# First gathers ahead of the decode root, tile 0 turned beside the decode output, and a new order of the last sums

## The chip, the cores and the metric

The kernel runs as one program on 1 core of a Trainium2 chip. The metric is the device time of an execution in microseconds. TensorE (PE) multiplies; PEld is its loading of stationary operands; VectorE (DVE), ScalarE (ACT) and GpSimd (POOL) work elementwise; SyncE (SP) issues DMAs. Each engine runs its own instructions in order, and the engines meet at semaphores.

## What is computed

One step of a hybrid decoder layer for a prompt of 1024 tokens and 8 decode rows with 8192 cached positions each. What matters here is its second half:

```python
x = x + jnp.concatenate([attn, s5_out], axis=-1) @ w_out
x = x + hier_moe(rmsnorm(x, ln2_g), w_router_group, b_router_group, ...)
y_prompt = rmsnorm(xp, ln_f_g)          # and y_sample for the decode rows

# hier_moe: softmax over 4 groups, the best group; in it the best 2 of 8 experts
for e in range(N_EXPERTS):              # 32 experts, each 1024 -> 256 -> 1024
    he = jax.nn.silu(t @ w_gate[e]) * (t @ w_up[e])
    out = out + comb[:, e:e + 1] * (he @ w_down[e])
```

The attention of a decode row is normalized per head (the "decode root" below is its inverse square root), and the normalized and scaled heads go through `w_out`.

## The kernel before

The first part is a plan: `streams` lists units of work (such as `("V", ...)`, a group of cache pages), each with a cost and with the units it waits for. `make_plan` puts them in one order, and `banks` gives each unit that writes PSUM one of 6 banks in turn. Every engine then runs its part of the units in the plan's order, with a few moved by hand: `DVE_PLAN` and `POOL_PLAN` are these orders for VectorE and GpSimd, `PE_PLAN` for TensorE.

The plan ends thus. The prompt tokens are routed (`pick1`, `pick2`, `rank`, `rt0`, `rt1`, `ids`, `lists`, `spread`, `route`) while the last cache pages of the decode rows are read. `route` on VectorE writes `idc`, the row numbers of the first tiles, and signals `s_route`. The decode rows come last: `ov` 7, `dout` (the heads' sums of squares; `root` on GpSimd, L576, raises them to -0.5), `dout2` (scaled heads into `xm`), `out` NT (product with `w_out` on TensorE, L1856, added on VectorE at L1491), `hn` (mean square on ScalarE and VectorE, root on GpSimd), `hs` (L1504: normalized rows into `h2`), `hT` (8 turns on TensorE at L2182, copied with the ln2 scale on VectorE at L1512 beside the 96 rows of expert tile 0 and of tile 1).

The experts run in steps of one tile each: 96 gathered token rows and the 8 decode rows, through one expert. GpSimd gathers rows from `h2_scratch` with three indirect DMAs (`gather`, L694) into `hg[v % 2]`; VectorE turns and scales them (`scale`, L1749 and L1752) into `hgT[v % 2]`; TensorE multiplies gate and up (16 matmul instructions of 512 columns); ScalarE takes the tanh (L974); VectorE finishes the gated product (L1774, L1776); TensorE turns it (L2249) and multiplies down (8 instructions). Weights of a tile are loaded by SyncE (L529, L530) into one of four buffers as soon as the down product of the tile four before has read it. Tile v of the first round is `gather(0, v)` and `scale(0, v)`.

Before the change the first list is `lists` in GpSimd's order, put right behind `dout`: it waits for pages, clears `hg[0]` (L707), drains, waits for `s_route` and gathers tile 0. Tile 1 is gathered after all units (L722 to L726): wait for all pages, clear `hg[1]` (L723), drain, gather. On VectorE `turn0` (= `scale(0, 0)`) stands behind `hs` of the decode rows, and so ahead of their `hT`. `scale(0, 1)` follows all units.

At the end the two expert outputs of each token lie in `y_scratch`. SyncE waits for `s_stored` (ScalarE's signal that all scatters have landed) and loads tile after tile (L548, two loads of 512 KB each, 8 tiles of 128 tokens). For each, `combine` adds the weighted outputs to the residual `x1`: VectorE with two instructions (L1825) in tiles 0, 1, 4, 7 and the decode rows; for tiles 2, 3, 5 and 6 (`on_pe`) TensorE sums them with diagonal weights (4 matmuls of 512 columns, which are 8 instructions) and VectorE adds the sum (L1820). ScalarE squares, VectorE takes the mean, GpSimd the root (L749), VectorE normalizes (`normed`, L1838), SyncE stores (L552, L554). All engines take the tiles in the order 0 to 8, where 8 is the decode rows.

Of the kernel before, what the change touches and what calls it, by code (L numbers as in the profile page):

```python
# [9 lines left out]
NT = SEQ // 128  # L10
# [49 lines left out]
def psum_keys(unit):  # L60
# [18 lines left out]
        "dout": [(("dss",), 1)], "dout2": [(("drep",), 1)], "rank": [(("rank",), 1)], "ids": [(("ids",), 1)], "spread": [(("sp",), 1)],  # L79
# [3 lines left out]
def streams():  # L83

    dec = [(("dprep",), 2.5, [(("dq",), 6.0)])]
    for x in range(NPASS):
# [6 lines left out]
        for y in range(SPP):  # L93
# [9 lines left out]
            (("out", NT), 4.0, [(("dout2",), 1.0), (("out", NT - 1, 1, 1), 0.0)]), (("hn", NT), 0.0, [(("out", NT), 2.0)]),  # L103
# [151 lines left out]
def hymba_step(nc, io):  # L255
# [29 lines left out]
    with ctx:  # L285
# [120 lines left out]
        on_pe = [2, 3, 5, 6]  # L406
# [87 lines left out]
        def _(sp):  # L494
# [50 lines left out]
            sp.wait_ge(s_stored, 1)  # L545
            for i in range(NT):
                for c in range(2):
                    sp.dma_start(yg[i][c], io["y_scratch"][SEQ * c + 128 * i:SEQ * c + 128 * i + 128, :]).then_inc(f_g[i], 16)  # L548
            for i in range(NT + 1):
                sp.wait_ge(f_out, i + 1)  # L550
# [8 lines left out]
        def _(gp):  # L559
# [145 lines left out]
            def lists():  # L705
# [8 lines left out]
            todo = {"stats": stats, "dprep": dprep, "dkv": dkv, "dk2": dk2, "u": u, "k": k, "v": v, "O": O, "dout": dout,  # L714
                    "bU": bU, "bK": bK, "bH": bH, "bS": bS, "ld1": ld1, "ld2": ld2, "ld3": ld3, "hn": hn, "hs": hs,
                    "route": lists}
# [29 lines left out]
            def inv_rms(i):  # L746
                gp.wait_ge(f_ms, i + 1)
# [3 lines left out]
            for i in range(NT + 1):  # L751
                inv_rms(i)
# [10 lines left out]
        def _(act):  # L763
# [250 lines left out]
            for i in range(NT + 1):  # L1014
                act.wait_ge(f_x, i + 1)
                r = 128 if i < NT else NB
                act.activation(yb[i % 2][0:r, :], x1[0:r, i, :], ACT.Square, accum_out=st[0:r, i:i + 1]).then_inc(f_sq, 1)
# [3 lines left out]
        def _(dve):  # L1021
# [808 lines left out]
            def mean(i):  # L1830
                dve.wait_ge(f_sq, i + 1)
# [3 lines left out]
            def normed(i):  # L1835
                r = 128 if i < NT else NB
                dve.wait_ge(f_rs, i + 1)
# [4 lines left out]
            for i in range(NT + 1):  # L1842
# [5 lines left out]
            mean(NT)  # L1848
            normed(NT - 1)
            normed(NT)  # L1850


        @block.tensor
        def _(pe):
# [339 lines left out]

            def rank_():
# [210 lines left out]
```

## Time and profile before

| | us |
|---|---|
| median of 3 runs (lowest to highest) | 1426.63 (1423.94 to 1430.79) |
| profiled execution | 1422.35 |
| its span | 1420.7 |
| TensorE busy | 1261.7 (89%) |
| VectorE busy | 566.6 (40%) |
| GpSimd busy | 284.9 (20%) |
| ScalarE busy | 247.1 (17%) |

The profile has one line for a group of instructions: start and length in us, engine, line of the kernel, operation, the tile written and the tiles read, their shapes and the count; in square brackets how long the engine sat idle before, and what ended that. "PEclk" is the clock that TensorE was granted, 1.00 being 2.4 GHz and 0.50 being 1.2 GHz. Lengths of matmuls are modelled at their ends. Its mean over the execution is 0.949.

### The profile page before, as it was taken

The numbers are of one execution on the slowest core, as the hardware profiler recorded it, in microseconds if no ns is written. First come the engines' busy times: TensorE is split into PE (matmuls) and PEld (weight loads), VectorE is DVE, ScalarE is ACT, GpSimd is POOL, SyncE is SP. The second block draws the span as 40 slices with busy tenths as digits, with TensorE's granted clock in tenths as the row PEclk, the third lists the DMA queues.
The fourth block names the chain that finished last, engine by engine and source line by source line (L and its number), as shares of the span: only waits on it lengthen the run. The fifth ranks groups of instructions, "written<-read, shape, count | busy, mean of one in ns | idle before, by whom it ended". The sixth has DMA issues, their size and how long they took to land.

```text
span 1420.7 us, 26426 instructions
## 1 busy us (share of the span) xinstructions
PE 1261.7 (89%) x8778; PEld 633.6 (45%) x8778; DVE 566.6 (40%) x1452; ACT 247.1 (17%) x476; POOL 284.9 (20%) x395
## 2 busy tenths in 40 slices
PE   7999898999869988998887999996699999999944
PEld 4545565654324435666663444433234443443411
DVE  2723535343374556454441111216253332333317
ACT  3101121131112323332320100000011111111112
POOL 2003231232200200000010000000334544444311
PEclk9999999999999999999899999996699999999987
DMA  9998989778977999999998899899959999999736
GB/s 372 324 336 270 338 263 308 259 219 308 330 249 243 316 372 336 384 326 331 314 356 331 294 307 318 306 343 326 370 202 344 355 362 350 355 363 345 286 123 256
DMA packets 184178, 443.66 MB, mean 312 GB/s; under 512 B 26453, under 2 KB 26897, under 8 KB 175506
## 3 DMA queue, kind: packets, MB, share of 16 engines
q1 hardware_dynamic: 163602, 390.21, 77.4%
q0 software_dynamic: 20480, 52.12, 10.3%
q8 instruction: 66, 1.08, 0.3%
q14 instruction: 30, 0.25, 0.1%
HBM read 418.77 MB, written 30.65 MB: 316 GB/s over the span
## 4 chain that ended last, share of the span: by engine, by line
PE 67%; DMA 12%; issue 8%; DVE 5%; SPq 4%; DVEq 1%; POOL 1%; ACT 1%; POOLq 0%; ACTq 0%
PE WA L1856 52%; PE SC L1856 7%; PE OD L1856 5%; DMA ring<-in_cacheK 5%; SPq L513 4%; DMA ring<-in_cacheV 3%; DMA ring<-h_scratch,idc 2%; DMA arena<-in_x_s 2%; PE WA L1975 1%; DVE st L1163 1%; DMA arena<-y_scratch 1%; DVE arena L1838 1%; PE WA L2182 0%; DMA rope<-in_rope 0%; DVE arena L1179 0%
## 5 line engine op out<-in xcount | busy, mean ns | idle before, releaser
L1856 PE MATMUL WA<-arena 128*104 128x512 f32 (+11 forms) x1440 | 350.2, 427 | 21.9 <-issue 7.2
L1856 PE MATMUL WA<-arena,xm 128*128 128x512 f32 (+3 forms) x828 | 320.4, 582 | 8.4 <-DMA arena<-in_w_out 6.6
L1856 PEld LDWEIGHTS WA<-arena 64*128 64x128 f32 (+4 forms) x1440 | 182.6, 187 | 173.2 <-issue 149.5
L1856 PEld LDWEIGHTS WA<-arena,xm 128*128 128x128 f32 (+1 forms) x828 | 127.1, 175 | 165.6 <-issue 157.3
L576 POOL TENSOR_TENSOR st<-st,consts 128x1 f32<-128x1 f32 (+2 forms) x18 | 13.7, 763 | 499.1 <-DVEq L1197 279.2
L1856 PE MATMUL WA<-xm,arena 128*128 128x512 f32 (+1 forms) x192 | 87.0, 601 | 1.7 <-ACT arena L979 1.3
L1856 PE MATMUL OD<-ring,sall 128*32 128x512 f32 x512 | 69.5, 653 | 17.4 <-DMA ring<-in_cacheV 17.4
L1856 PE MATMUL OD<-ring,qpad 128*32 128x128 f32 x2048 | 66.3, 280 | 11.5 <-DMA ring<-in_cacheK 11.4
L1856 PE MATMUL SC<-ring,qpad 128*32 128x128 f32 x2048 | 65.1, 279 | 8.9 <-DMA ring<-in_cacheK 8.8
L1856 PEld LDWEIGHTS OD<-ring,qpad 128*32 128x32 f32 x2048 | 55.1, 112 | 31.6 <-issue 16.5
L1856 PEld LDWEIGHTS SC<-ring,qpad 128*32 128x32 f32 x2048 | 55.1, 112 | 24.4 <-issue 12.0
L1856 PE MATMUL SC<-ring,sall 128*32 128x512 f32 x512 | 61.4, 598 | 1.5 <-DMA ring<-in_cacheV 1.5
L849 ACT ACTIVATE arena<-WA,st 128x128 f32<-128x128 f32 (+7 forms) x64 | 47.4, 740 | 80.0 <-DVEq L1167 78.0
L1856 PE MATMUL WA<-xm 128*104 128x512 f32 (+1 forms) x132 | 58.3, 593 | 0.0
L1749 DVE STREAM_TRANSPOSE xm<-ring 128x768 f32<-128x768 f32 x16 | 25.1, 1570 | 83.0 <-DMA ring<-h_scratch,idc 83.0
L1856 PE MATMUL WA<-ring,xm 128*104 128x512 f32 x128 | 57.7, 605 | 0.0
L694 POOL DMA_INDIRECT ring<-h_scratch,idc x48 | 52.0, 1082 | 22.3 <-issue 17.6
L1485 DVE TENSOR_TENSOR arena<-arena,WA 128x512 f32<-128x512 f32 x16 | 11.0, 688 | 111.7 <-PE WA L1856 86.3
L694 POOL DMA_INDIRECT qpad<-h_scratch,idc x48 | 51.1, 1065 | 21.6 <-issue 21.6
L1856 PEld LDWEIGHTS WA<-xm,arena 128*128 128x128 f32 (+1 forms) x192 | 34.7, 186 | 45.9 <-issue 44.4
L1749 DVE STREAM_TRANSPOSE arena<-qpad 128x768 f32<-128x768 f32 x16 | 25.1, 1567 | 68.9 <-DMA qpad<-h_scratch,idc 68.9
L1163 DVE TENSOR_REDUCE st<-WA 128x1 f32<-128x128 f32 (+7 forms) x64 | 48.5, 758 | 5.1 <-issue 0.4
(372 smaller groups left out, 1238.8 us busy)
## 6 DMA issues: line engine op xcount, KB each, us to landing
ring<-in_cacheK SPq DMA_DIRECT2D x512, 256.0 KB, 4.6
ring<-in_cacheV SPq DMA_DIRECT2D x512, 256.0 KB, 4.7
arena<-in_w_gu SPq DMA_DIRECT2D x16, 2048.0 KB, 8.8
arena<-in_w_dn SPq DMA_DIRECT2D x16, 1024.0 KB, 11.8
ring<-in_w_gu SPq DMA_DIRECT2D x8, 2048.0 KB
xm<-in_w_gu SPq DMA_DIRECT2D x8, 2048.0 KB, 9.5
ring<-in_w_dn SPq DMA_DIRECT2D x8, 1024.0 KB
xm<-in_w_dn SPq DMA_DIRECT2D x8, 1024.0 KB, 13.1
```

The source lines that it names most:

```text
L513: sp.dma_start(ring[:, GRP * half + j, :], cache[bass.ds(pages[j], 1), :, :] .rearrange("a p n -> p (a n)")).then_inc(s_pg[PARTS * half + ...
L576: gp.tensor_tensor(x, x, consts[0:x.shape[0], C_NH:C_NH + 1].to_broadcast(list(x.shape)), ALU.pow).then_inc(s_rs, 1)
L694: gp.indirect_dma_start(hg[v % 2][:, 256 * b:256 * b + 256], None, io["h2_scratch"], bass.IndirectOffsetOnAxis(ap=idc[:, 3 * v + b:3 * v + ...
L849: act.activation(P[:, n % 2, c, 0:w], slot("S", i, h, c)[:, 0:w], ACT.Exp, bias=st[:, 4 * (n % 2) + c:4 * (n % 2) + c + 1], scale=HD ** -0 ...
L1163: dve.reduce_max(st[:, 8 + c:9 + c], S[:, 0:w], AX)
L1485: dve.tensor_tensor(q, q, slot("o", i, a)[:, :], ADD)
L1749: dve.transpose(rows_.rearrange("p k (b j) -> p k b j", b=3), hg[v % 2].rearrange("p (b j k) -> p k b j", b=3, k=KD)).then_inc(m_T, 1)
L1838: dve.scalar_tensor_tensor(x1[0:r, i, :], x1[0:r, i, :], st[0:r, i:i + 1], lnf[0:r, :], MUL, MUL)\
L1856: return pe.matmul(out, lhsT, rhs, start=first, stop=last, **kw)
L1975: last = pe.transpose(slot("AT", i, h)[:, 128 * j:128 * j + 128], P[:, n % 2, 0, 128 * j:128 * j + 128], ident)
```

## The change

Four edits and what belongs to them. (1) GpSimd takes the first list where the plan has `route`, ahead of `dout`; the list for tile 1 becomes a unit `next` right behind `dout`, without the drain: a semaphore says when the clearing is done. (2) VectorE takes `turn0` right behind `dout2`, ahead of the decode output's add. (3) A new unit `warm` puts five matmuls of identity by constants behind the decode output's product on TensorE, into a bank of its own (it counts as 4.0 us in the plan), and five more stand before the last sums, after the load of tile 0. Their results are not used. (4) The last tiles run in the order `TAIL` on all engines, and SyncE waits for the scatters itself in place of `s_stored`. The banks of the units behind `warm` stay what they were, as a unit of two banks follows it and starts at an even bank either way.

```diff
-            (("out", NT), 4.0, [...]), (("hn", NT), 0.0, [(("out", NT), 2.0)]),
+            (("out", NT), 4.0, [...]), (("warm",), 4.0, [(("out", NT), 0.0)]), (("hn", NT), 0.0, [(("out", NT), 2.0)]),
...
-                {("lists",): [u, ("route",)], ("hs", NT): [u, ("turn0",)]}.get(u, [u])]
-
-    POOL_PLAN = [x for u in PLAN if u != ("route",) for x in ([u, ("route",)] if u == ("dout",) else [u])]
+                {("lists",): [u, ("route",)], ("dout2",): [u, ("turn0",)]}.get(u, [u])]
+
+    POOL_PLAN = [x for u in PLAN for x in ([u, ("next",)] if u == ("dout",) else [u])]
...
-        on_pe = [2, 3, 5, 6]
+        on_pe, TAIL = [2, 3, 5, 6], [0, 1, 4, 2, 3, 5, 6, 7, NT]
...
-            sp.wait_ge(s_stored, 1)
-            for i in range(NT):
+            for n in range(2):
+                sp.wait_ge(m_st[n], 32 * n4)
+            for i in TAIL[:NT]:
...
+            def second():
+                gp.wait_ge(s_pgfree, RING // QP + NB * 2 * NPAGE // QP)
+                gp.memset(hg[1], 0.0).then_inc(s_qbd, 1)
+                gp.wait_ge(s_qbd, 4)
+                gather(0, 1)
+
...
-            gp.wait_ge(s_pgfree, RING // QP + NB * 2 * NPAGE // QP)
-            gp.memset(hg[1], 0.0)
-            gp.drain()
-            gather(0, 1)
...
-            for i in range(NT + 1):
+            for n, i in enumerate(TAIL):
                 combine(i)
-                if i >= 1:
-                    mean(i - 1)
-                if i >= 2:
-                    normed(i - 2)
...
+                if n >= 1:
+                    mean(TAIL[n - 1])
+                if n >= 2:
+                    normed(TAIL[n - 2])
...
+            def warm():
+
+                vacant(pe, "warm")
+                for n in range(5):
+                    last = mm(slot("warm")[:, :], ident, consts[:, 0:512])
+                    if n == 0:
+                        last.then_inc(full_sem("warm"), 1)
+                last.then_inc(free_sem("warm"), 1)
+
...
+
+            pe.wait_ge(f_g[0], 48)
+            for n in range(5):
+                mm(W[2][:, 0:512], ident, consts[:, 0:512])
             for n, i in enumerate(on_pe):
```

The waits and counts of ScalarE, VectorE, GpSimd and TensorE in the tail go by a tile's place in `TAIL` accordingly.

## Rows read from the trace of the kernel before

**Rows 1.** Chain of waits, steady expert steps: start us, us, what
```profile
1046.48 10.30 PE WA L1856 x24
...
1056.97 10.30 PE WA L1856 x24
```

**Rows 2.** Timeline by start: end of prompt rows, decode root, first expert
```profile
948.94 0.75 DVE L1504 TENSOR_SCALAR arena<-arena,st 128x1024 f32<-128x1024 f32 x1 [0.71 <-POOL st L576]
...
1002.21 0.56 POOL L576 TENSOR_TENSOR st<-st,consts 32x1 f32<-32x1 f32 x1 [51.61 <-DVEq L1259]
...
1011.29 1.70 DVE L1491 TENSOR_TENSOR arena<-arena,WA 8x256 f32<-8x256 f32 x4 [6.43 <-PE WA L1856]
...
1015.19 1.20 DVE L1504 TENSOR_SCALAR arena<-arena,st 8x1024 f32<-8x1024 f32 x1 [0.72 <-POOL st L576]
...
1016.48 1.04 PE L2182 MATMUL WA<-consts,arena 8*128 8x8 f32 x8 [5.33 <-DVEq L1505]
...
1021.14 0.22 DVE L1512 TENSOR_TENSOR arena<-WA,colw 128x64 f32<-128x64 f32 x1
...
1021.54 9.84 PE L1856 MATMUL WA<-arena 128*104 128x512 f32 x16 [4.02 <-DVEq L1515]
```

**Rows 3.** Timeline: route, first gathers, turn of tile 0
```profile
996.73 0.17 DVE L1740 CAST idc<-qpad 128x12 uint32<-128x12 f32 x1
...
1008.59 1.13 POOL L694 DMA_INDIRECT qpad<-h_scratch,idc  x1 [5.13 <-issue]
...
1011.35 1.01 POOL L694 DMA_INDIRECT qpad<-h_scratch,idc  x1 [0.30 <-issue]
...
1018.50 1.55 DVE L1749 STREAM_TRANSPOSE arena<-qpad 128x768 f32<-128x768 f32 x1 [2.11 <-DMA qpad<-h_scratch,idc]
...
1020.77 1.22 POOL L694 DMA_INDIRECT ring<-h_scratch,idc  x1 [0.31 <-issue]
```

**Rows 4.** Timeline of the tail: sums of the last tiles
```profile
1379.05 2.65 DVE L1825 SCALAR_TENSOR_TENSOR arena<-arena,wts 128x1024 f32<-128x1024 f32 x2 [18.31 <-DMA arena<-y_scratch]
...
1385.57 2.05 PE L1856 MATMUL WA<-arena,ring 128*128 128x512 f32 x2 [17.76 <-DMA arena<-y_scratch]
...
1390.91 1.22 DVE L1820 TENSOR_TENSOR arena<-arena,WA 128x1024 f32<-128x1024 f32 x1 [4.69 <-PE WA L1856]
...
1404.27 1.22 DVE L1820 TENSOR_TENSOR arena<-arena,WA 128x1024 f32<-128x1024 f32 x1
...
1415.91 2.47 DVE L1838 SCALAR_TENSOR_TENSOR arena<-arena,st 128x1024 f32<-128x1024 f32 x2
```

**Rows 5.** Windows of 1 us: window, length, busy per engine, granted clock, DMA, GB/s
```profile
1010.00:1011.00 1.00, 1.00 (x23) 0.32 (x12) 0.00 (x0) 0.00 (x0) 0.97 (x1) 1.00 0.90 385
...
1014.00:1015.00 1.00, 0.00 (x0) 0.00 (x0) 0.15 (x1) 0.29 (x2) 0.41 (x1) 0.50 1.06 402
...
1034.00:1035.00 1.00, 0.98 (x3) 0.69 (x4) 0.77 (x1) 0.34 (x1) 0.90 (x1) 0.50 0.43 123
```

**Rows 6.** Timeline: first gated product and second gate and up product
```profile
1031.41 0.38 ACT L974 ACTIVATE arena<-WA 104x256 f32<-104x256 f32 x1 [17.12 <-PE WA L1856]
...
1032.96 0.41 DVE L1774 SCALAR_TENSOR_TENSOR arena<-arena,WA 104x256 f32<-104x256 f32 x1
...
1034.39 8.48 PE L1856 MATMUL WA<-ring,xm 128*104 128x512 f32 x16
```

**Rows 7.** Load at 1377.4 of source line L548: its instruction and landing time
```profile
L548 SPq DMA_DIRECT2D arena<-y_scratch x1: 458/458/458, 1377.4 to 1377.4; - x1
...
DMA to landing us min/median/max: 10.5/10.5/10.5
```

**Rows 8.** All gathers, source line L694: time to landing
```profile
DMA to landing us min/median/max: 2.1/6.8/11.8
```

**Rows 9.** Timeline of SyncE: weight issues of two steps in the loop
```profile
1203.72 0.33 SPq L529 DMA_DIRECT2D xm<-in_w_gu  x1
...
1215.49 0.34 SPq L529 DMA_DIRECT2D arena<-in_w_gu  x1
```

More of the change, by code:

```diff
@@ L78, in psum_keys @@
         "hT": [(("hT",) + a, 2)], "r": [(("r",) + a, 1)],
-        "dout": [(("dss",), 1)], "dout2": [(("drep",), 1)], "rank": [(("rank",), 1)], "ids": [(("ids",), 1)], "spread": [(("sp",), 1)],
+        "dout": [(("dss",), 1)], "dout2": [(("drep",), 1)], "rank": [(("rank",), 1)], "ids": [(("ids",), 1)], "spread": [(("sp",), 1)], "warm": [(("warm",), 1)],
     }.get(k, [])
@@ L102, in streams @@
     dec += [(("dout",), 0.1, [(("ov", NB - 1), 1.0)]), (("dout2",), 0.2, [(("dout",), 2.0)]),
-            (("out", NT), 4.0, [(("dout2",), 1.0), (("out", NT - 1, 1, 1), 0.0)]), (("hn", NT), 0.0, [(("out", NT), 2.0)]),
+            (("out", NT), 4.0, [(("dout2",), 1.0), (("out", NT - 1, 1, 1), 0.0)]), (("warm",), 4.0, [(("out", NT), 0.0)]), (("hn", NT), 0.0, [(("out", NT), 2.0)]),
             (("hs", NT), 0.0, [(("hn", NT), 2.5)]), (("hT", NT), 1.0, [(("hs", NT), 0.8)]),
@@ L712, in lists @@
                 gather(0, 0)
+            def second():
[3 more added lines that the diff above has]
+                gather(0, 1)
             todo = {"stats": stats, "dprep": dprep, "dkv": dkv, "dk2": dk2, "u": u, "k": k, "v": v, "O": O, "dout": dout,
                     "bU": bU, "bK": bK, "bH": bH, "bS": bS, "ld1": ld1, "ld2": ld2, "ld3": ld3, "hn": hn, "hs": hs,
-                    "route": lists}
+                    "route": lists, "next": second}
             for unit in POOL_PLAN:
@@ L746, in inv_rms @@
             def inv_rms(i):
-                gp.wait_ge(f_ms, i + 1)
+                gp.wait_ge(f_ms, TAIL.index(i) + 1)
                 x = st[:, i:i + 1]
                 gp.tensor_tensor(x, x, consts[:, C_NH:C_NH + 1], ALU.pow).then_inc(f_rs, 1)
-            for i in range(NT + 1):
+            for i in TAIL:
                 inv_rms(i)
@@ L1011, in _ @@
             act.nop().then_inc(s_stored, 1)
-            for i in range(NT + 1):
-                act.wait_ge(f_x, i + 1)
+            for n, i in enumerate(TAIL):
+                act.wait_ge(f_x, n + 1)
                 r = 128 if i < NT else NB
-                act.activation(yb[i % 2][0:r, :], x1[0:r, i, :], ACT.Square, accum_out=st[0:r, i:i + 1]).then_inc(f_sq, 1)
+                act.activation(yb[n % 2][0:r, :], x1[0:r, i, :], ACT.Square, accum_out=st[0:r, i:i + 1]).then_inc(f_sq, 1)
         @block.vector
@@ L1841, in _ @@
             dve.wait_ge(f_gf, 16)
-            for i in range(NT + 1):
+            for n, i in enumerate(TAIL):
                 combine(i)
-                if i >= 1:
-                    mean(i - 1)
-                if i >= 2:
-                    normed(i - 2)
-            mean(NT)
-            normed(NT - 1)
-            normed(NT)
+                if n >= 1:
+                    mean(TAIL[n - 1])
+                if n >= 2:
+                    normed(TAIL[n - 2])
+            mean(TAIL[NT])
+            normed(TAIL[NT - 1])
+            normed(TAIL[NT])
         @block.tensor
@@ L2231, in _ @@
                     "dout": dout, "dout2": dout2, "bP": bP, "bK": bK, "bX": bX, "bY": bY, "glu": glu, "out": out_, "hT": hT,
-                    "r": r_, "rank": rank_, "ids": ids_, "spread": spread}
+                    "r": r_, "rank": rank_, "ids": ids_, "spread": spread, "warm": warm}
             for unit in PE_PLAN:
```

8 lines of the change are left out of this document (4 added, 4 removed).

## The prediction

> **What bounds the kernel now.** I read the 40 slices of the page first: TensorE is busy nearly throughout, and the change works where it is not: in the stretch from about 990 to 1046 us between the last pages of the cache and the steady run of experts, and in the last 50 us. The chain of waits then shows what stands between: from 1046 us on it is TensorE alone, 24 matmuls of 512 columns in 10.30 us each step, 0.43 us apiece [rows 1], so every microsecond by which the first step starts sooner should reach the end. Ahead of it I followed the timeline by engine. The decode root's chain is a row of short steps over all engines: GpSimd's power at 1002.21, the output product of the 8 decode rows, whose result VectorE adds from 1011.29, GpSimd's power again, the normalized rows (L1504, 1015.19, 1.20 us), eight turns on TensorE from 1016.48 for 1.04 us, then VectorE's copy at 1021.14 and the first expert's gate and up product at 1021.54 [rows 2]. Between 1017.52 and 1021.14 that chain stands still. Its engine, VectorE, is turning expert tile 0 from 1018.50 (`turn0`), and that waited for gathers of which the first went out at 1008.59 only [rows 3]. So the late gather sets the start of the experts. The tail is a chain on VectorE: it sits idle 4.69 us before 1390.91 for TensorE's sum of tile 2, and from there to the end it hardly rests [rows 4].
>
> **Gathers ahead of the decode root, and the turn beside the output product.** The route is ready at 996.90 (end of the cast into `idc`), yet GpSimd takes the first list after the root at 1002.21, then clears the target, and the gather starts 5.13 us after the clearing [rows 3]. After the change the clearing is done long before the route is there (GpSimd idles 51.61 us before 1002.21 [rows 2]), and GpSimd waits at the route. I take its start at 997.5. The last of three gathers began 1011.35 - 1008.59 = 2.76 us after the first and took 1.01 [rows 3], so they end near 1001.3, and the root at 1002.21 isn't held. The turn began 9.9 us after the first gather's start (1008.59 to 1018.50) [rows 3], and weights filled the queues then as they will now; so it can begin at 1007.4. It lasts with its scaling 2.64 us (1018.50 to 1021.14) [rows 2, 3], to 1010.1, before the product's result at 1011.29. Its cover is VectorE's idle time of 6.43 us before that row [rows 2]. VectorE's copy then follows the turns on TensorE directly: 1017.52 + 0.10 = 1017.62 in place of 1021.14, **3.52 us** sooner. The second list's clearing and gathers stand where the first ones stood; its stall of 5.13 us goes too if it belongs to the drain, which this list no longer has. Nobody needs it before the first gate and up product ends.
>
> **A clearing that leaves the chain.** L1504 took 0.75 us for 128 rows of 1024 at 948.94, but 1.20 for 8 rows at 1015.19 [rows 2], while GpSimd cleared the second target (it starts right after the power that released L1504). That clearing now runs right behind the first power. I count **0.45 us**. The Trainium skill, SBUF — State Buffer, section Who interferes with whom, says that VectorE in its two-port modes and GpSimd hold one port pair exclusively, and the trace agrees with these 0.45 us. By the same page the change has a debit: the second gathers, from about 1004, run beside the root's last small VectorE steps, and if a gather held the pair, one of 1.01 us could be added and the sum would be 9.4. The row at hand shows the gather and not VectorE lengthened (1.22 for 1.01) [rows 3], so I add nothing.
>
> **Five matmuls behind the output product (`warm`).** The granted clock is 1.00 (2.4 GHz) when that product ends and 0.50 (1.2 GHz) at 1014 after idling; the first gate and up product then takes 9.84 us for 16 matmuls, where 16 x 0.43 = 6.88 [rows 2, 5]. The clock is at 0.50 again at 1034, and the second product takes 8.48 [rows 5, 6]. `warm` is 10 matmul instructions, 4.3 us at the high clock, from 1011.2 to 1015.5, inside the wait for L1504, and delays nothing; at the low clock it would be 8.6 us to 1019.8, and the eight turns would be 3.3 us late. I take the first since the clock was high there. Most is saved if the clock then stays: 9.84 - 6.88 = **2.96**, and 8.48 - 6.88 = **1.60** for the second product. Between `warm` and the first product about 2 us remain with little in them, and 2 us between the two products; one fall costs what the second product shows, 1.60. I count one: **-1.60**.
>
> **The second tile is no longer waited for.** VectorE turned tile 1 when its gather landed, and only after it took the gated product: ScalarE's tanh began at 1031.41 and lasted 0.38, but L1774 ran at 1032.96 [rows 6]. With tile 1 turned before 1021, L1774 can follow 0.47 us after the tanh's start, at 1031.88: **1.08 us**.
>
> Head: 3.52 + 0.45 + 2.96 + 1.60 - 1.60 + 1.08 = 8.0 us. Bounds: no fall 9.6; two falls 6.4. The steps after it are TensorE's at 10.48 each and pass it on. The weights are asked for by the step itself, and tiles 2 and 3 are asked for at the same event as before.
>
> **The tail.** TensorE's sum of tile 2 began at 1385.57 at the low clock (the first two matmuls 2.05 us), and VectorE had it at 1390.91: 5.34 us, where 8 x 0.43 + 0.2 = 3.64 [rows 4]. In the new order tile 2 is loaded fourth. The load in that place (its second half issued 1377.4, landed after 10.5) is there at 1387.9 [rows 7], so TensorE starts 2.3 us later than now. Tile 0 is there at 1379.0, and the new five matmuls run from then, 4.3 us at the high and 8.6 at the low clock, so they end by 1387.6, before the load. If the clock is high then, VectorE has tile 2 at 1391.5, tiles 3, 5 and 6 each 3.44 later, tile 6 at 1401.85 instead of 1404.27 [rows 4]: **2.4 us**. VectorE fills the wait with tile 4 (two steps, 2.65 us), which it no longer does between tiles 3 and 5; what is left behind tile 6 is the same work as before (14.1 us, to 1418.38). With the low clock at the start 1.7 us of it go back: 0.7. Letting SyncE wait for the scatters itself saves one hop, under 0.1, taken as nothing.
>
> Sum: 8.0 + 2.4 = 10.4 us. The profiled execution, 1422.35 (span 1420.7), would come to 1411.9. It lies 4.3 us under the median of the runs, 1426.63; taken from that, 10.4 gives **1416.2**.
>
> **Rivals.** *The clock isn't kept* at either place: `warm` ends 2 us too soon and the tail's matmuls stop before tile 2 is there. Head 3.52 + 0.45 + 1.08, tail 0.7: 5.8 us, 1420.9. For it: the clock fell within 3 us of the output product's end [rows 5]. Against it: the gap left is shorter. *The root queues behind the gathers*: the stall of 5.13 us comes with the first gather and not with the drain, so the gathers end at 1006.3 and the power is 4.1 us late: 6.3 us gained, 1420.3. Against it: later gathers follow at once. *The turn blocks the output*: VectorE waits in `turn0` with the decode output behind it. A gather landed after 11.8 us at most [rows 8]; from 1000.2 that is 1012.0, the add starts at 1014.65, 3.4 late: 7.0 gained, 1419.6. It is also the case in which the change doesn't do what it says. *Slower*: steady steps miss their gathers. The step that asked for weights at 1203.72 was followed by the next at 1215.49, 11.77 us and not 10.48, as its tile had landed late [rows 9]. If the new start moved gathers against weight bursts, each missed step costs 1.29; from 8 missed steps of some 28 the gain is gone, and 20 give 25.8 - 10.4 = 15.4 us more, 1442.0. Against it: gathers and weights are both issued by the step, so their distance in time doesn't move.
>
> **How the numbers follow.** Forecast 0.60 (1414 to 1419), clock not kept 0.20, root queued 0.06, turn blocked 0.08, missed steps 0.06. A change under about 0.5% (7.1 us) can't be told from none here; the limit is 1419.5. The forecast's case lies mostly below it, the middle three mostly above: faster 0.64, same 0.30, slower 0.06. Range: no fall and a little luck of the runs, 12.0 + 2.7, gives 1411.5; above, the clock rival plus the scatter of runs, 1423.5.
>
> **What would show it.** In the changed profile: the first gather before the power at the decode root; the turn of tile 0 over before the output's add; L1504 at 0.75; the first gate and up product starting some 6.4 us after the output's add begins (now 10.25), near 7 us long; steps of 10.48; VectorE's tile 4 directly behind tile 1, and tile 6 about 2.4 us sooner after the first load than now. A root power that starts late, a turn after the add, or clock 0.50 in the first product or in tile 2 would each prove a step wrong.

## The result and the profile after

Eight runs of the changed kernel have a median of 1415.95 us (1405.94 to 1426.02), eight of the kernel before, on the same chip, 1429.33 (1423.94 to 1433.97). The medians are 13.4 us apart. The ratio, taken run by run, is 0.9917, with a 95% interval of 0.9889 to 0.9945: some 12 us faster, clear of none and well under 2%. The profiled execution took 1418.66 us, its span is 1417.0 and its mean granted clock 0.951; that span is only 3.7 us under the one of before. A slower stretch in front of the change hides the rest, and has to come off first.

The timeline of the changed kernel, from the route to the second gate and up product (start us, us, engine, line, operation, tile written and read, shapes, count, and in brackets the idle time before and what ended it):

```profile
1002.99 0.17 DVE L1744 CAST idc<-qpad 128x12 uint32<-128x12 f32 x1
...
1004.07 1.11 POOL L696 DMA_INDIRECT qpad<-h_scratch,idc  x1 [46.59 <-DVEq L1745]
...
1008.73 0.57 POOL L578 TENSOR_TENSOR st<-st,consts 32x1 f32<-32x1 f32 x1 [0.92 <-DVEq L1263]
1009.26 0.73 POOL L718 MEMSET ring<- 128x768 f32 x1
1009.33 0.69 DVE L1268 TENSOR_SCALAR rt<-consts,st 32x32 f32<-32x32 f32 x1 [0.72 <-POOL st L578]
...
1010.76 1.04 POOL L696 DMA_INDIRECT ring<-h_scratch,idc  x1 [0.77 <-POOL ring L718]
...
1013.20 1.59 DVE L1753 STREAM_TRANSPOSE arena<-qpad 128x768 f32<-128x768 f32 x1 [1.81 <-DMA qpad<-h_scratch,idc]
...
1017.51 4.56 PE L1860 MATMUL WA<-consts 128*128 128x512 f32 x10
1017.73 1.70 DVE L1495 TENSOR_TENSOR arena<-arena,WA 8x256 f32<-8x256 f32 x4 [1.88 <-PE WA L1860]
...
1021.63 0.74 DVE L1508 TENSOR_SCALAR arena<-arena,st 8x1024 f32<-8x1024 f32 x1 [0.72 <-POOL st L578]
1022.45 1.04 PE L2186 MATMUL WA<-consts,arena 8*128 8x8 f32 x8 [0.38 <-DVEq L1509]
...
1023.53 0.23 DVE L1516 TENSOR_TENSOR arena<-WA,colw 128x64 f32<-128x64 f32 x1 [1.16 <-PE WA L2186]
1023.94 7.11 PE L1860 MATMUL WA<-arena 128*104 128x512 f32 x16 [0.45 <-DVEq L1519]
...
1031.09 0.38 ACT L978 ACTIVATE arena<-WA 104x256 f32<-104x256 f32 x1 [10.36 <-PE WA L1860]
...
1031.58 0.41 DVE L1778 SCALAR_TENSOR_TENSOR arena<-arena,WA 104x256 f32<-104x256 f32 x1
```

Line numbers are shifted against before, by 4 in the lines of VectorE: its L1504 is L1508 here, L1740 is L1744, L1774 is L1778 (TensorE's L1856 is L1860, its L2249 is L2262; SyncE's L529 is L530). Three things are to be seen. The first gather stands ahead of the power of the decode root, and the turn of tile 0 (1013.20) ahead of the output's add (1017.73). Nothing waits any more between the eight turns on TensorE and VectorE's copy (1022.45, 1023.53); before it was 4.66 us from the one's start to the other's [rows 2]. And the product takes 7.11 us, not 9.84.

Now the stretch in front. The cast into `idc` ends at 1003.16 here and at 996.90 before [rows 3]. The change isn't the cause. Up to that point it moves one instruction only, the clearing of tile 0's target, and the rows in front of that are late already: L1504 for the last prompt rows started at 948.94 before [rows 2], its L1508 starts 6.13 us later:

```profile
955.07 0.75 DVE L1508 TENSOR_SCALAR arena<-arena,st 128x1024 f32<-128x1024 f32 x1 [0.71 <-POOL st L578]
...
956.73 0.76 POOL L709 MEMSET qpad<- 128x768 f32 x1
```

In the profiles of all kernels in this study the cast ended between 996.90 and 1015.63 us after the span's start. So all that follows is counted from the end of the cast ("C+"), and the tail from the start of the first addition of tile 0 ("F+"). A profile alone would have put the gain at 3.7 us.

| event | before | after |
|---|---|---|
| power of the decode root starts | C+5.31 | C+5.57 |
| turn of tile 0 starts | C+21.60 | C+10.04 |
| scaling of the decode rows (L1504, now L1508) starts | C+18.29 | C+18.47 |
| first gate and up product starts | C+24.64 | C+20.78 |
| second gate and up product starts | C+37.49 | C+29.68 |
| weights of the first steady step asked for | C+49.57 | C+40.32 |
| 27 steps, to the last such request | 284.90 | 283.99 |
| last request to F | 47.68 | 47.52 |
| TensorE's sum of tile 2 starts | F+6.52 | F+9.86 |
| VectorE adds tile 2 | F+11.86 | F+15.30 |
| VectorE adds tile 6 | F+25.22 | F+25.60 |
| end of the span | F+41.65 | F+42.01 |

The head gained 9.25 us, the steps 0.91, the last stretch in front of the tail 0.16, the tail lost about 0.4, and the stretch in front of the cast took 6.26: 9.25 + 0.91 + 0.16 - 0.36 - 6.26 = 3.7, the difference of the spans. Counted so, the change is worth 10.0 us in the profile. The steady steps are as before, in the chain of waits of the changed kernel (start us, us, what):

```profile
1054.27 10.30 PE WA L1860 x24
1064.57 0.18 PE OD L2262 x2
1064.76 10.30 PE WA L1860 x24
```

The step that came late before [rows 9] comes late again, 11.12 us from one request to the next for 11.77. Before, a second one took 11.04; here it takes 10.48, and the first takes 10.78 instead. These three differences are the 0.91 us of the steps. Which steps come late changes from profile to profile, in two kernels none does, so I don't put them down to the change. Timeline of SyncE:

```profile
1201.03 0.33 SPq L530 DMA_DIRECT2D xm<-in_w_gu  x1
...
1212.15 0.34 SPq L530 DMA_DIRECT2D arena<-in_w_gu  x1
```

The tail of the changed kernel, and the clock around it (windows: length; busy time of TensorE, of its weight loads, of VectorE, ScalarE and GpSimd; granted clock, DMA share, GB/s):

```profile
1374.99 2.65 DVE L1829 SCALAR_TENSOR_TENSOR arena<-arena,wts 128x1024 f32<-128x1024 f32 x2 [18.15 <-DMA arena<-y_scratch]
1375.03 6.07 PE L1860 MATMUL WA<-consts 128*128 128x512 f32 x10 [11.12 <-DMA arena<-y_scratch]
...
1384.85 2.00 PE L1860 MATMUL WA<-arena,ring 128*128 128x512 f32 x2 [3.76 <-DMA arena<-y_scratch]
...
1390.29 1.22 DVE L1824 TENSOR_TENSOR arena<-arena,WA 128x1024 f32<-128x1024 f32 x1 [3.40 <-PE WA L1860]
...
1400.59 1.22 DVE L1824 TENSOR_TENSOR arena<-arena,WA 128x1024 f32<-128x1024 f32 x1 [0.54 <-PE WA L1860]
```

```profile
1384.00:1385.00 1.00, 0.15 (x1) 0.15 (x2) 1.00 (x1) 0.00 (x0) 0.00 (x0) 0.98 1.00 410
1385.00:1386.00 1.00, 1.00 (x2) 0.48 (x3) 0.71 (x3) 0.72 (x1) 0.40 (x1) 0.50 1.03 422
```

The new order is there: VectorE adds tile 6 10.3 us after tile 2 (13.36 before). But tile 2 itself comes 3.44 us later, for two reasons that the rows show: its load lands later, and after a pause of 3.76 us TensorE's clock goes from 0.98 in the microsecond in which the sum begins to 0.50 in the next.

### The profile page after: what moved, and what is told of

It reads as the page before. It is cut to its first block, busy times and chain, and to the rows that moved or that the text cites. A ratio compares the mean times of both kernels' runs of the same rounds, so it can differ in the third digit from the quotient of the medians.

```text
span 1417.0 us, 26467 instructions
## 1 busy us (share of the span) xinstructions
PE 1270.1 (90%) x8798; PEld 637.7 (45%) x8798; DVE 566.3 (40%) x1452; ACT 247.3 (17%) x476; POOL 285.3 (20%) x395
## 3 DMA queue, kind: packets, MB, share of 16 engines
q8 instruction: 66, 1.08, 0.3%
## 4 chain that ended last, share of the span: by engine, by line
PE 71%; DMA 11%; SPq 6%; DVE 5%; issue 4%; DVEq 2%; ACT 1%; POOL 1%; ACTq 0%; POOLq 0%
PE WA L1860 54%; PE SC L1860 7%; PE OD L1860 7%; DMA ring<-in_cacheK 6%; SPq L514 5%; DMA ring<-in_cacheV 2%; PE WA L1979 1%; DMA arena<-y_scratch 1%; DMA ring<-h_scratch,idc 1%; DMA qpad<-h_scratch,idc 1%; PE WA L2186 1%; SPq L508 0%; DMA rope<-in_rope 0%; DVE st L1167 0%; DVE arena L1842 0%
## 5 line engine op out<-in xcount | busy, mean ns | idle before, releaser
L1860 PE MATMUL WA<-arena 128*104 128x512 f32 (+11 forms) x1440 | 344.8, 426 | 15.4 <-issue 6.2
L1860 PE MATMUL WA<-arena,xm 128*128 128x512 f32 (+3 forms) x828 | 320.9, 582 | 8.2 <-DMA arena<-in_w_out 6.4
L1860 PEld LDWEIGHTS WA<-arena 64*128 64x128 f32 (+4 forms) x1440 | 181.3, 188 | 163.6 <-issue 146.4
L1860 PEld LDWEIGHTS WA<-arena,xm 128*128 128x128 f32 (+1 forms) x828 | 127.1, 175 | 166.3 <-issue 158.1
L1860 PE MATMUL WA<-xm,arena 128*128 128x512 f32 (+1 forms) x192 | 86.9, 600 | 1.7 <-ACT arena L983 1.3
L1860 PE MATMUL OD<-ring,qpad 128*32 128x128 f32 x2048 | 68.8, 286 | 19.4 <-DMA ring<-in_cacheK 19.4
L1860 PE MATMUL OD<-ring,sall 128*32 128x512 f32 x512 | 71.3, 672 | 14.7 <-DMA ring<-in_cacheV 14.7
L1860 PEld LDWEIGHTS OD<-ring,qpad 128*32 128x32 f32 x2048 | 56.5, 114 | 40.4 <-DMA ring<-in_cacheK 24.0
L1860 PE MATMUL SC<-ring,qpad 128*32 128x128 f32 x2048 | 64.3, 276 | 9.3 <-DMA ring<-in_cacheK 9.3
L1860 PEld LDWEIGHTS SC<-ring,qpad 128*32 128x32 f32 x2048 | 54.6, 111 | 24.8 <-DMA ring<-in_cacheK 12.1
L1860 PE MATMUL SC<-ring,sall 128*32 128x512 f32 x512 | 61.4, 598 | 2.0 <-DMA ring<-in_cacheV 2.0
L1860 PE MATMUL WA<-xm 128*104 128x512 f32 (+1 forms) x132 | 58.3, 592 | 0.0
L1860 PE MATMUL WA<-ring,xm 128*104 128x512 f32 x128 | 56.3, 592 | 0.0
L1860 PEld LDWEIGHTS WA<-xm,arena 128*128 128x128 f32 (+1 forms) x192 | 34.6, 185 | 45.9 <-issue 44.4
```

The costliest lines, as they stand in the source:

```text
L1860: return pe.matmul(out, lhsT, rhs, start=first, stop=last, **kw)
```

## Experiments

All compare with the changed kernel unless said. Where a median and a ratio stand, the kernel was run against the kernel before on the same chip; the others are one profiled execution each. What rests on one profile is to be read with its scatter: heads and tails of the same instructions differ by up to 3 us.

### The head alone, and the tail alone

```diff
-        on_pe, TAIL = [2, 3, 5, 6], [0, 1, 4, 2, 3, 5, 6, 7, NT]
+        on_pe, TAIL = [2, 3, 5, 6], [0, 1, 2, 3, 4, 5, 6, 7, NT]
...
-            pe.wait_ge(f_g[0], 48)
-            for n in range(5):
-                mm(W[2][:, 0:512], ident, consts[:, 0:512])
```

> The change's head part alone: lists, turn and warm as in the change, the last tiles in the old order 0 to 8 and without the five matmuls before the last sums. Theory 1, the head carries everything: from the end of the cast into idc to the first steady weight issue 40.3 us as in the change (before 49.6), from the first add of tile 0 to the last normalizing 39.3 us as before, total about 9 us under before (ratio 0.993 to 0.994), equal to the change or slightly faster. Rival, the prediction's own sum: tail worth 2.4 us, so this kernel is 2.4 us slower than the change and 8 us faster than before.

Median 1418.64 us, ratio 0.9931, interval 0.9894 to 0.9968. The first steady request stands at C+40.33, as in the change (40.32), and the tail is that of before: the span ends at F+41.46.

The other half has the head of the kernel before (its order of lists and turn, its drain, no `warm`), and the tail of the change:

```diff
-                {("lists",): [u, ("route",)], ("dout2",): [u, ("turn0",)]}.get(u, [u])]
+                {("lists",): [u, ("route",)], ("hs", NT): [u, ("turn0",)]}.get(u, [u])]
...
-    POOL_PLAN = [x for u in PLAN for x in ([u, ("next",)] if u == ("dout",) else [u])]
+    POOL_PLAN = [x for u in PLAN if u != ("route",) for x in ([u, ("route",)] if u == ("dout",) else [u])] + [("next",)]
```

> The change's tail alone (order 0, 1, 4, 2, 3, 5, 6, 7, decode rows, five matmuls after tile 0 is loaded, SyncE waiting for the scatters), head as before. Theory 1: the tail is worth nothing, since tile 2 is loaded one place later and the clock has fallen again by then: first add to last normalizing 39.0 to 40.0 us (before 39.3), total within 1 us of before, ratio 0.999 to 1.001. Rival, the prediction: 36.9 us and a total 2.4 us under before, ratio 0.998. In the head: cast into idc to first steady weight issue 49.6 us as before, give or take 2 by the clock.

Median 1426.79, ratio 0.9995, interval 0.9967 to 1.0023. In the times the tail brings nothing that can be measured, and the head can't be told from the whole change; but the interval is 4 us wide to each side, so the times don't rule out the 2.4 us that were forecast. In the tail's profile the clock was kept at tile 2 and the span ended at F+39.80, 1.85 us sooner than before. So where the clock happens to hold, this tail has some 2 us, and it held in one of the four profiles with the new order and five matmuls (table below). Its head, which should have been as before (49.6 us give or take 2), had its first steady request at C+46.89: one profile of a head is good to some 3 us.

### The parts of the head

**The five matmuls taken out** (with the old order of the last sums, the tail's five kept):

```diff
-            (("out", NT), 4.0, [...]), (("warm",), 4.0, [(("out", NT), 0.0)]), (("hn", NT), 0.0, [(("out", NT), 2.0)]),
+            (("out", NT), 4.0, [...]), (("hn", NT), 0.0, [(("out", NT), 2.0)]),
```

> Two questions in kernels that don't touch: in the head the matmuls behind the decode output are left out, in the tail the five matmuls stay but the order is the old 0 to 8. Head: if these matmuls keep the clock, the first gate and up product takes 9 to 10 us instead of 7.1 and the second 7 to 8.5, so cast into idc to first steady weight issue is 43 to 45 us; if the clock would have been kept anyway, 40.3. Tail: tile 2's load is there 6.4 us after tile 0's and the five matmuls take 6.1, so tile 2 should be summed at the high clock and reach VectorE 10.1 us after the first add (before 11.9, change 15.3); then VectorE is the bound and first add to last normalizing is 37.6 us. If VectorE isn't the bound in the old order, less than 1 us is gained.

The first product in its profile, and the clock in it:

```profile
1025.22 10.12 PE L1860 MATMUL WA<-arena 128*104 128x512 f32 x16 [0.45 <-DVEq L1519]
```

```profile
1030.00:1031.00 1.00, 1.00 (x2) 0.30 (x1) 0.00 (x0) 0.00 (x0) 0.91 (x1) 0.50 1.06 397
1032.00:1033.00 1.00, 1.00 (x3) 0.34 (x2) 0.00 (x0) 0.00 (x0) 0.41 (x1) 1.00 1.07 434
```

The product begins in its place, C+20.83, and takes 10.12 us for 7.11; the first steady request is at C+43.36. So `warm` is worth 3.0 us, all of it in the first product (2.96 in the prediction). The second product takes 7.03 us here too: its shortening from 8.48 isn't the work of `warm`. The tail of this kernel, old order with five matmuls, ends at F+40.15.

**The five matmuls alone**, in the head of before (the plan as in the tail-alone kernel, `warm` kept, eight matmuls in the tail):

> The head of before (lists, turn and drain in their old places) with only the five matmuls behind the decode output's product. Theory: alone they save little, since the first gate and up product then starts 24 us after the end of the cast, 8 us behind them, and the clock has fallen: it takes 9 to 10 us and the steady weight issue comes at 47 to 50. Rival: they are worth the 3.0 us that they are worth in the change (40.33 against 43.36 without them), so 44 to 46. Tail: order of the change with eight matmuls: 38.0 us again.

```profile
1014.21 4.56 PE L1860 MATMUL WA<-consts 128*128 128x512 f32 x10
...
1023.91 10.11 PE L1860 MATMUL WA<-arena 128*104 128x512 f32 x16 [2.07 <-DVEq L1519]
```

The product starts at C+23.59 and takes 10.11 us, and the first steady request stands at C+48.63, between the two other heads of the old kind (49.57 before, 46.89 in the tail-alone kernel). `warm` ends at 1018.77, the product comes 5.1 us later, and the clock is at 0.50 again. This first product is no shorter than one without `warm` (9.84 before, 9.47 in the tail-alone kernel). Alone it is worth nothing: it lives from the short way to the product that the early turn gives (1.9 us in the change, 1022.07 to 1023.94).

**The turn put back** behind the scaling of the decode rows:

```diff
-                {("lists",): [u, ("route",)], ("dout2",): [u, ("turn0",)]}.get(u, [u])]
+                {("lists",): [u, ("route",)], ("hs", NT): [u, ("turn0",)]}.get(u, [u])]
```

> The kernel of the change with one part undone: tile 0's turn stands again behind the scaling of the decode rows (in front of the copy of their transpose, as before), where the change has it behind the decode's second output product. Theory: the turn's three transposes take 1.6 us of VectorE and are ready 10 us after the end of the cast into idc; in the old place they lie between the decode rows and the copy of hT, so the copy ends about 1.4 to 1.7 us later (21.8 to 22.1 after the end of the cast instead of 20.4), the first gate and up product begins at 22.2 to 22.5 instead of 20.8, and the first weight issue of the steady steps at 41.7 to 42.0 instead of 40.3. Rival one: the turn in its new place delays the decode rows as much as it frees behind them (it waits for the gathers while the sum of the decode output could run); then the first product begins at 20.8 as in the change. Rival two: TensorE's clock falls in the longer pause in front of the product, and then the product takes 8 to 10 us instead of 7.1 and the steady steps begin 43 or more after the cast. No other part of the kernel is altered.

```profile
1022.00 0.74 DVE L1508 TENSOR_SCALAR arena<-arena,st 8x1024 f32<-8x1024 f32 x1 [0.72 <-POOL st L578]
...
1022.86 1.58 DVE L1753 STREAM_TRANSPOSE arena<-qpad 128x768 f32<-128x768 f32 x1
...
1025.92 8.81 PE L1860 MATMUL WA<-arena 128*104 128x512 f32 x16 [2.06 <-DVEq L1519]
```

The product starts at C+22.38, 1.60 us later than in the change, as the theory said, and then takes 8.81 us, as its second rival said: both are true. The first steady request is at C+43.62, 3.3 us later. So of the 3.86 us by which the product starts sooner, the turn's new place gives 1.60, and the early lists 2.26, with the 0.46 by which L1508 is shorter in them; the turn's place also keeps the clock.

**The second tile's list behind the decode rows' norm** (no matmuls in the tail here):

```diff
-    POOL_PLAN = [x for u in PLAN for x in ([u, ("next",)] if u == ("dout",) else [u])]
+    POOL_PLAN = [x for u in PLAN for x in ([u, ("next",)] if u == ("hn", NT) else [u])]
```

> The change with the list of tile 1 behind the decode rows' last power in place of behind the decode root's, and in the tail without the five matmuls before the last sums. Head: the clearing runs beside L1504 again. If the two engines share a port there (theory), L1504 takes 1.20 us again, not 0.74, and the first gate and up product starts 0.45 us later, 21.2 us after the end of the cast into idc instead of 20.8. Tile 1's first gather goes out near 19.5 us instead of 7.6 and is turned near 30.5; the first gate and up product ends at 28.0, so VectorE's gated product waits for that turn and TensorE's first turn comes at 33 to 34 us instead of 29.5, with the first steady weight issue 4 us later or more, 44 to 46. Rival: the place of this list is free, steady issue at 40.8. Tail: tile 2's sum at the low clock, VectorE has it 14.5 to 15.3 us after the first add, tail 39 to 40 us.

```profile
1004.41 0.23 DVE L1268 TENSOR_SCALAR rt<-consts,st 32x32 f32<-32x32 f32 x1 [0.72 <-POOL st L578]
...
1016.46 0.73 POOL L718 MEMSET ring<- 128x768 f32 x1
1016.53 1.20 DVE L1508 TENSOR_SCALAR arena<-arena,st 8x1024 f32<-8x1024 f32 x1 [0.69 <-POOL st L578]
...
1026.45 0.38 ACT L978 ACTIVATE arena<-WA 104x256 f32<-104x256 f32 x1 [10.79 <-PE WA L1860]
...
1030.02 1.55 DVE L1753 STREAM_TRANSPOSE xm<-ring 128x768 f32<-128x768 f32 x1 [10.48 <-DMA ring<-h_scratch,idc]
...
1032.67 0.41 DVE L1778 SCALAR_TENSOR_TENSOR arena<-arena,WA 104x256 f32<-104x256 f32 x1
```

This run taught the most. The first product starts at C+20.76 and takes 7.11 us, and yet the first steady request is at C+48.57, 8.25 us after the change's and 1 us ahead of before's. VectorE stands 10.48 us at the turn of tile 1, whose gathers had just been issued; tile 0's gated product lies queued behind that turn and starts 6.2 us after the tanh (0.49 in the change, 1031.09 to 1031.58). The idle TensorE then starts the second product with the clock down (9.40 us for 7.03). So the early product is worth next to nothing without the early second list. I had expected 4 us or more, C+44 to 46, and priced it too low. The upper rows show the other term: L1508 takes 1.20 us while GpSimd clears beside it, 0.74 when it doesn't. The product was to come 0.45 us later for it and didn't: L1268 lost its own collision (0.23 us for 0.69) and the output's add starts at C+14.11 for C+14.56, so this clearing costs VectorE 0.46 us at either place.

**The drain kept** ahead of the second list, in its new place:

```diff
-                gp.memset(hg[1], 0.0).then_inc(s_qbd, 1)
-                gp.wait_ge(s_qbd, 4)
+                gp.memset(hg[1], 0.0)
+                gp.drain()
```

> The change with the drain left in the list of tile 1 (clear, drain, gather), behind the decode root's power. If the drain is what held the gathers by 5.13 and 3.57 us before, the first gather of tile 1 goes out 3.5 to 5 us after the clearing, at 10.5 to 12 us after the end of the cast instead of 7.6. If it was the first gather's own start, the change would have had it at its first gather too, which went out 0.91 us after the cast. Either way the decode rows' power at 17.9 us isn't held and tile 1 has landed before its turn at 21.9, so the first steady weight issue stays at 40.3 us. Tail as in the change: 37.5 to 39.7 us, by whether the clock is high when tile 2's sum starts.

```profile
1006.71 0.73 POOL L718 MEMSET ring<- 128x768 f32 x1
...
1012.04 1.04 POOL L696 DMA_INDIRECT ring<-h_scratch,idc  x1 [4.60 <-issue]
...
1020.38 0.74 DVE L1508 TENSOR_SCALAR arena<-arena,st 8x1024 f32<-8x1024 f32 x1 [0.72 <-POOL st L578]
```

The drain costs GpSimd 4.60 us where the wait on the semaphore costs 0.77. Nobody needed these 3.8 us: VectorE turns tile 1 only after its copies, with nothing to wait for, at C+22.86 (21.86 in the change). The first steady request was expected unchanged and came at C+42.92, 2.6 us later; 1.0 of it is an output add that waited 2.70 us for something that the trace doesn't name, 1.6 a first product of 8.71 us with the clock down in part. The second goes with the first: TensorE stood 2.42 us in front of the eight turns for 0.38, and the product came 3.9 us after `warm` for 1.9. The late add can't be tied to the drain from one profile. The two kernels with the old head and the new tail have it too (C+15.34 and 15.29, 14.38 before); its cause stays open.

**The gathers next to the root.** GpSimd clears and drains only once the route is there, so that the root queues behind it (the tail has the old order, five matmuls, and one normalizing step moved ahead):

```diff
-                gp.memset(hg[0], 0.0)
-                gp.drain()
                 gp.wait_ge(s_route, 1)
+                gp.memset(hg[0], 0.0)
+                gp.drain()
```

> The change with the clearing and the drain of the first list behind the wait for the route, so that its gathers run where the decode root's power is due. Theory (the root queues behind them on GpSimd): first gather near 5 us after the end of the cast instead of 0.9, the third ends near 9, the root's power starts near 9 instead of 5.57, and everything behind it is 3 to 4 us later: first gate and up product at 24 to 25 us, steady weight issue near 44. Rival: the drain is short when nothing is in flight, and the power is held by less than 1 us. Tail: old order 0 to 8, five matmuls after tile 0's load, and tile 0 normalized ahead of the sum of tile 2, in VectorE's wait; if VectorE is the bound there (36.7 us with the old order and the matmuls), 1.3 us less, 35.4; if TensorE is, 36.7.

```profile
999.51 0.73 POOL L710 MEMSET qpad<- 128x768 f32 x1 [46.81 <-DVEq L1745]
...
1005.35 1.11 POOL L696 DMA_INDIRECT qpad<-h_scratch,idc  x1 [5.11 <-issue]
...
1009.12 0.59 POOL L578 TENSOR_TENSOR st<-st,consts 32x1 f32<-32x1 f32 x1
```

The root starts at C+9.77 (5.57 in the change), the product at C+24.95 (20.78), the first steady request at C+44.48 (40.32): 4.2 us at the root, 4.2 at the end of the head. What holds the root reaches the end in full. The rival of the prediction (4.1 us) is priced right, and only the clearing and the drain standing ahead of the route kept it away. In the tail the step moved ahead brought nothing: from the first addition to the end of the last normalizing it took 38.6 us where 35.4 to 36.7 were expected; without that step, in the same order and with the same matmuls, it took 37.9 and 38.5.

### The parts of the tail

**Eight matmuls for five:**

> The change with eight matmuls of identity in place of five after tile 0 is loaded. Theory 1 (the clock had fallen to 0.50 when tile 2's sum began at 1384.98): they last 8.7 us and end 1.2 us before tile 2 is there, the clock stays 1.00, tile 2's sum takes 3.6 us instead of 5.4, and first add to last normalizing is 38.0 us instead of 39.7. Rival: the late load alone holds the tail, then tile 2 reaches VectorE no sooner than 15.3 us after the first add and the tail stays at 39.7 us.

```profile
1373.89 9.00 PE L1860 MATMUL WA<-consts 128*128 128x512 f32 x16 [11.12 <-DMA arena<-y_scratch]
...
1383.76 1.13 PE L1860 MATMUL WA<-arena,ring 128*128 128x512 f32 x2 [0.86 <-DMA arena<-y_scratch]
```

TensorE's pause ahead of tile 2 shrinks to 0.86 us, the clock stays at 1.00, and the tail ends at F+40.34 instead of 42.01. Median 1416.37, ratio 0.9937, interval 0.9902 to 0.9973: 1.7 us in the profile, not to be seen in the times.

**The old order with the five matmuls:**

> The kernel of the change with its head and its five products ahead of the last sums, but the last sums in the order of before (0, 1, 2, 3, ... 8), so that VectorE sums tile 4 between the TensorE tiles. Theory: the new order gives nothing by itself, since the chain is paced by TensorE's sum of tile 2, which waits for its load. In the old order tile 2 is loaded as the third of eight and not as the fourth, so its sum begins 6.5 to 7.4 us after the first addition of tile 0 (9.3 to 9.9 in the new order) and its addition comes at about 10.3 to 11.1 with the clock high; tile 6's follows 13.4 later, at 23.7 to 24.5, and the end of the span 16.4 after that, 40.1 to 40.9 us after the first addition, against 42.0 in the change's profile and 40.2 to 40.3 where eight products precede the sums. The ratio to the kernel before is then 0.991 to 0.993, no different from the change's 0.992. Rival: the new order is worth its 1.2 us or more, and this kernel's ratio is 0.993 or more with its end at 41.5 or later.

```profile
1370.09 6.42 PE L1860 MATMUL WA<-consts 128*128 128x512 f32 x10 [11.16 <-DMA arena<-y_scratch]
...
1377.35 1.12 PE L1860 MATMUL WA<-arena,ring 128*128 128x512 f32 x2 [0.84 <-DMA arena<-y_scratch]
...
1381.09 1.22 DVE L1824 TENSOR_TENSOR arena<-arena,WA 128x1024 f32<-128x1024 f32 x1 [4.50 <-PE WA L1860]
```

Tile 2 starts at F+7.29 and is added at F+11.03; tile 6 follows 13.4 later at F+24.38, and the span ends at F+40.74, all inside what was expected. The ratio, 0.9965 with 0.9929 to 1.0002, is above the 0.991 to 0.993 that I had given; its interval reaches into it. It also covers the head alone (0.9931). The times can't rank these kernels.

The ends of the span over all profiles, by what the tail is and what TensorE's pause ahead of tile 2 was:

| order | matmuls | pause us | clock at tile 2 | end |
|---|---|---|---|---|
| old | 0 | 17.76, 17.42 | low | F+41.65 (before), 41.46 |
| old | 5 | 1.42, 0.84, 0.21 | high | F+40.84, 40.74, 40.15 |
| new | 0 | 20.33 | low | F+41.08 |
| new | 5 | 3.76, 3.76, 3.55 | low | F+42.01 (after), 41.87, 41.65 |
| new | 5 | 1.99 | high | F+39.80 |
| new | 8 | 0.86, 0.17 | high | F+40.34, 40.18 |

From the addition of tile 6 to the end it is 16.35 to 16.44 us in every one. The new order shortens tile 2 to tile 6 by 3.1 us and delays tile 2 by about as much (F+13.07 to 13.64 for F+10.43 to 11.10 at the high clock, F+14.37 to 15.30 for F+11.66 to 11.86 at the low); between the lows and the highs of one order lie 0.6 to 2.2 us. With five matmuls the old order had short pauses and the high clock in all three profiles, the new order in one of four. At the high clock the ends of the two orders overlap (F+39.80 to 40.34 new, 40.15 to 40.84 old), so what this tail can gain comes from the matmuls; that the order adds to it isn't shown.

## Why the prediction was right, and where not

The time (1416.2 forecast, 1415.95 measured) and the mechanism in the head were right. That the two times lie 0.25 us apart is luck: the median of before that I started from was 2.7 us lower than that of all eight runs, and the gain came out larger than 10.4 (13.4 us by the medians; 0.0083 x 1429.33 = 11.9 by the ratio), and the two made up for each other. The sum of 10.4 us came out nearly whole in the profiles too (10.0 with the 0.91 of the steps, 8.9 without), but its parts didn't: the head gave 9.25 for 8.0 and the tail lost 0.36 where it was to give 2.4. The head's 9.25 are 3.86 by which the first product starts sooner, 2.73 by which it is shorter, 1.22 between the two products and 1.45 in the second.

- **Gathers and turn, 3.52, and the clearing, 0.45.** Product start: 24.64 - 20.78 = 3.86, against 3.97. The first gather begins 0.91 after the cast and not 0.6, and the power of the root 0.26 later than before; the turn was done before the add. L1508 took 0.74. Both terms hold against the one profile of before. The three profiles of a head with the old order (49.57, 48.63 with `warm`, 46.89) differ by 2.7 us: in the second and third tile 0's gathers had landed when VectorE came to the turn (0.12 us of waiting for 2.11), and their first product starts 1.0 us sooner; the rest is the clock. Taken against their mean, 48.36, the head's gain is 8.0, and 6.6 against the lowest.
- **`warm`, 2.96 + 1.60 - 1.60.** The first product fell from 9.84 to 7.11 us: 2.73, and 3.0 with the matmuls alone taken out. The second fell from 8.48 to 7.03: 1.45, but it did so without `warm` as well, so that term belongs to the shorter pause in front of it. The one fall of the clock that I had counted (-1.60) didn't come: the changed kernel and three others with its head had the clock at 1.00 through both products (first steady request C+40.32, 40.33, 40.35 and 39.77). That is the term that was mis-sized in the head. The other side of it: `warm` is no independent term. Alone it gave nothing that can be seen.
- **The second tile, 1.08.** The gated product follows the tanh after 0.49 for 1.55 us: 1.06. As a difference it holds. As a price of the edit it misleads: without the early second list the whole gain of the head is gone, all but 1 us in the profile. I had made a sum of terms out of what is a chain of covers. The list of tile 1 in its old place was late by 1.08 us as long as the first product was late too; once the product comes 3.9 us sooner and is 2.7 shorter, the list is what ends last.
- **The tail, 2.4.** The failed step is "If the clock is high then", and the start of tile 2 before it. The load gave F+9.86 for F+8.85 (9.23 to 9.90 in the kernels with the new order). The five matmuls, of 6.07 us, ended 3.76 us ahead of it; I had only checked that they end *before* the load, and they end too long before. With tile 2 added 5.44 us after its start and not 3.6, 1.0 + 1.8 = 2.8 us go back, which is all of the 2.4. The low-clock case that I had priced at 0.7 was the nearer one, and still 1.1 us too good, by the later load. Why the load in the fourth place landed 1.0 us later than the fourth of before, counted from F, is open.
- **The stall of 5.13 us** belongs to the drain, as assumed: 4.60 with it, 0.77 without, in the same place. It is no fixed length, though (last section).
- **The debit that I set to nothing.** I read [rows 3] as a gather that grew beside VectorE and left VectorE alone. VectorE did grow: its copy of 128 x 64 beside that gather (L1516, 1021.57) took 0.41 us, and 0.19 in the changed kernel, where it falls between two gathers. In the change the second gather of tile 0 lengthens a step in front of the root by 0.22 us (last section); that is most of the 0.26 by which the root starts later.
- **Rivals.** The clock was kept in the head and lost in the tail; the root didn't queue; the turn didn't block the output (it waited 1.81 us for its gathers and ended before the add). The missed steps: 27 steps took 284.90 us before and 283.99 after; one was newly late, the first, by 0.30 us. The lower end of the range was added up wrongly: 1426.63 - 12.0 - 2.7 is 1411.9 and not 1411.5.
- **The profiled execution** was to come to 1411.9 and came to 1418.66: 6.26 us of that is the stretch ahead of the cast.

## What to carry to other kernels

When several steps meet at one point, a gain is a property of the set: price each edit also with the others in place, and ask of every step that was "early enough" whether it is so at the new time (here a list put late ate 8 of 9 us in its profile). Matmuls that only hold the clock are worth something where real work follows them closely; place them against the arrival that ends the wait, not against the one that begins it. And before two profiles are compared by their spans, find the last point that the change can't touch and count from there.

## What the runs showed of the hardware

- A drain on GpSimd between a clearing of 0.73 us and an indirect gather had no fixed price. GpSimd stood there 5.13 us (first list before, and in the two kernels with the old head), 5.11 and 4.60 (two experiments), 3.57 (second list before), and only 1.08 in the second list of the two kernels with the old head. With a semaphore wait for the same clearing it stood 0.77. What the drain waits for no run shows. The tail-alone kernel:

```profile
1018.51 1.05 POOL L696 DMA_INDIRECT ring<-h_scratch,idc  x1 [1.08 <-issue]
```

- VectorE's scaling of 8 x 1024 takes 1.20 us beside GpSimd's clearing of 128 x 768, and 0.74 without it, in every kernel that had one or the other. The same holds for a step that I hadn't looked at: L1268, 32 x 32 behind the decode root, takes 0.69 us in the change, where the second clearing now stands beside it (1009.26), and 0.23 us where none does (the run with the list behind the norm). Before, the first clearing stood there. So the change got rid of one such collision of two, and up to 0.46 us may still be had.
- The debit that the prediction took from the Trainium skill (SBUF — State Buffer, Who interferes with whom), that a gather could hold the port, showed too, in a place that I hadn't looked at and smaller than the 1.01 us named there. In the changed kernel, ahead of the root:

```profile
1005.49 1.01 POOL L696 DMA_INDIRECT qpad<-h_scratch,idc  x1 [0.30 <-issue]
...
1006.03 0.44 DVE L1250 TENSOR_SCALAR wmap<-wmap,mrow 128x4 f32<-128x4 f32 x1
```

L1250 takes 0.39 to 0.45 us in the five profiles in which it starts 0.54 us or more after this gather, and there the root's power starts at C+5.57. It takes 0.22 in the other seven: in three it starts 0.42 to 0.47 us after the gather, in four no gather runs beside it. L1274 takes 0.24 us beside a gather (1011.15) and the same without one. So a gather delays a small step of VectorE or not, by where in the gather the step falls.

- TensorE's clock after a pause in the tail: 0.50 in the three profiles with a pause of 3.55 to 3.76 us behind five matmuls and 1.00 in the six with 0.17 to 1.99. In the head the product behind `warm` ran at 1.00 when it came 1.9 to 2.3 us later, fell to 0.50 about 1 us after its start when it came 3.5 us later, and began low at 3.9 and 5.1 us.
- The end of the cast into `idc` moved by 18.7 us among profiles of kernels that differ up to there in no more than the place of one clearing (996.90 to 1015.63). The timed medians of the kernel before itself lay at 1429.33, 1430.02 and 1424.76 in three sets of runs. Against that a tail's 2 us can only be seen in profiles, by events counted from a near anchor.
